# Order of weight splits, norms and the second token tile at the ten block borders, and of the scan's first phases, in a one-core transformer forward pass

## The reference, cut to what matters

```python
x = layer_norm(ALPHA * x + (1.0 + gate) * y, g, b)      # borders mla, mlp0, s5, mlp1
h = x * (1.0 + scale) + shift                           # what the next block reads
x = x + MACARON_WEIGHT * rms_norm_2(swiglu(rms_norm_2(x, pre_g), ...), post_g)   # ffn blocks
# s5: u = h @ w_in; complex recurrence over 256 steps, 64 groups x 64 states
a = exp((lr + i*li) * dt);  s[t] = a * s[t-1] + B u[t];  y[t] = Re(C s[t]) + d * u[t]
z = gelu(y); out = (z * sigmoid(z @ w_glu + b_glu)) @ w_out
```

## Time and profile before

| what | value |
|---|---|
| median of 3 runs (lowest, highest) | 1851.33 us (1848.64, 1853.93) |
| the profiled execution, its own time | 1848.97 us |
| its span, first to last instruction | 1847.2 us |
| mean granted TensorE clock | 0.942 of full speed |
| busy in the span: PE, DVE, ACT, POOL | 91%, 61%, 45%, 8% |

### The profile page before, as it was taken

One profiled execution on the slowest core, in us unless ns is written; L12 is line 12 of the kernel. 1 busy time (PEld: TensorE's weight loads), 2 busy tenths in 40 slices (PEclk: granted clock), 3 DMA queues, 4 the chain that ended last, 5 costly groups with the idle time before them and its releaser, 6 DMA issues.

```text
span 1847.2 us, 20552 instructions
## 1 busy us (share of the span) xinstructions
PE 1679.6 (91%) x8247; PEld 1350.5 (73%) x8247; DVE 1135.9 (61%) x1346; ACT 834.3 (45%) x1129; POOL 144.3 (8%) x293
## 2 busy tenths in 40 slices
PE   8778899984989899989999959999999999789998
PEld 3656688863668688868888747888788888568887
DVE  1876767893989756585455756544655455655444
ACT  2443455543234445544444675343544344554343
POOL 4320010012631010000000000000000000000000
PEclk9878899997999899989999979999999999889999
DMA  9658368853019466536654524555456555225552
GB/s 299 236 161 255 133 235 309 296 208 114 2 38 334 153 219 247 175 111 206 221 198 161 194 71 171 192 183 192 150 182 205 183 193 194 91 92 204 183 184 90
DMA packets 165496, 335.45 MB, mean 182 GB/s; under 512 B 38773, under 2 KB 54461, under 8 KB 164250
## 3 DMA queue, kind: packets, MB, share of 16 engines
q1 hardware_dynamic: 144602, 292.63, 46.8%
q0 software_dynamic: 9696, 37.29, 5.5%
q10 hardware_dynamic: 11104, 4.23, 0.9%
HBM read 328.86 MB, written 6.83 MB: 182 GB/s over the span
## 4 chain that ended last, share of the span: by engine, by line
PE 69%; DVE 19%; ACT 4%; issue 3%; DMA 2%; POOL 2%; SPq 1%; DVEq 0%; ACTq 0%; POOLq 0%
PE ps L635 21%; PE ps L637 21%; PE ps L636 21%; DVE wlo L1715 5%; PE ps L720 2%; PE ps L1157 1%; ACT whi L1186 1%; SPq L532 1%; DVE work L1757 1%; DVE xlo L1720 1%; DVE work L2148 1%; DMA work<-in_mod_mix_w 1%; DVE X L1849 1%; DMA operands<-in_mod_ffn_w 1%; DVE small L1780 1%
## 5 line engine op out<-in xcount | busy, mean ns | idle before, releaser
L1715 DVE TENSOR_TENSOR wlo<-raw,whi 128x2048 fp32r<-128x2048 f32 (+2 forms) x247 | 559.4, 2284 | 303.0 <-ACT whi L1186 302.4
L1186 ACT ACTIVATE whi<-raw 128x2048 fp32r<-128x2048 f32 (+2 forms) x247 | 465.7, 1906 | 233.2 <-PE ps L637 185.8
L635 PE MATMUL ps<-whi,xhi 128*128 128x512 f32 (+2 forms) x1244 | 486.2, 391 | 26.3 <-DVE wlo L1715 15.3
L636 PE MATMUL ps<-wlo,xhi 128*128 128x512 f32 (+2 forms) x1244 | 478.7, 385 | 0.0
L637 PE MATMUL ps<-whi,xlo 128*128 128x512 f32 (+2 forms) x1244 | 478.6, 385 | 0.0
L635 PE MATMUL ps<-whi,hhi 128*128 128x512 f32 x736 | 295.5, 402 | 23.8 <-DVE hlo L1720 23.3
L635 PEld LDWEIGHTS ps<-whi,xhi 128*128 128x128 f32 x1244 | 240.5, 193 | 73.6 <-DVE wlo L1715 17.7
L636 PE MATMUL ps<-wlo,hhi 128*128 128x512 f32 x736 | 289.4, 393 | 0.0
L637 PE MATMUL ps<-whi,hlo 128*128 128x512 f32 x736 | 289.4, 393 | 0.0
L637 PEld LDWEIGHTS ps<-whi,xlo 128*128 128x128 f32 x1244 | 239.8, 193 | 45.7
L636 PEld LDWEIGHTS ps<-wlo,xhi 128*128 128x128 f32 x1244 | 240.8, 194 | 43.4
(11 more groups left out here) (347 smaller groups left out, 1610.8 us busy)
## 6 DMA issues: line engine op xcount, KB each, us to landing
raw<-in_mlp_w SPq DMA_DIRECT2D x64, 1024.0 KB, 5.3
raw<-in_ffn_w_gate SPq DMA_DIRECT2D x44, 1024.0 KB, 5.1
raw<-in_ffn_w_up SPq DMA_DIRECT2D x44, 1024.0 KB, 5.1
raw<-in_ffn_w_down SPq DMA_DIRECT2D x44, 1024.0 KB, 4.9
mod<-in_mod_ffn_w POOLq DMA_DIRECT2D x16, 1024.0 KB, 7.1
mod<-in_mod_mix_w POOLq DMA_DIRECT2D x12, 1024.0 KB, 6.6
work<-in_mod_mix_w SPq DMA_DIRECT2D x8, 1024.0 KB, 9.0
operands<-in_mod_ffn_w SPq DMA_DIRECT2D x8, 1024.0 KB, 8.1
```

What stands on the lines that cost most here:

```text
L635: pe.matmul(o, lh, rh, start=start, stop=False)
L636: pe.matmul(o, lh, rl, start=False, stop=False)
L1186: act.activation(whi[:, c % SPL, 0:n], raw[:, c % RAW, 0:n], ACT.Copy).then_inc(hi_done, 1)
L1715: dve.tensor_tensor(wlo[:, c % RAW, 0:n], raw[:, c % RAW, 0:n], whi[:, c % SPL, 0:n].bitcast(F32), ALU.subtract).then_inc(lo_done, 1)
```

## The change

At each border the split of the next block's first chunk moves ahead of the norm of tile 0 on DVE (and on ACT where it was not so), that of the third chunk ahead of the norm of tile 1, and PE takes head 2 of tile 0 before it transposes tile 1. In s5 POOL makes the phases of duos 0 and 1 before it opens the three row tiles, DVE ends phase 0 and phase 1 around `residual`, ACT makes tables 0 and 1 between its token copies, and the split of chunk c+6 goes into the scan's loop. PE transposes the first token slice before it spreads a modulation row (`spread_third`, L723). SP loads the two norm rows behind chunk c+8 instead of c+5.

```diff
-                if name == "s5" and k == 5:
+                if name == "s5" and k == 8:
                     sp.wait_ge(res_ok, 4)
...
                     head(nxt, 1, 0)
+                    head(nxt, 2, 0)
                     turn(nxt, 1)
-                    head(nxt, 2, 0)
...
                 acc_ready("s5", 1)
+                token_turn("s5", 0, 0)
                 spread_third(6, (0, 1))
-                for tt in range(T):
-                    token_turn("s5", 0, tt)
+                token_turn("s5", 0, 1)
...
# ACT, leave
+                hi(n0)
                 if name in ("mla", "s5"):
                     despread(2 if name == "mla" else 8)
-                if name in LN_GLUES: hi(n0); glue(0)  else: glue(0); hi(n0)
+                glue(0)
...
                 x_hi(nxt, 0)
-                if name in LN_GLUES: hi(n0 + 2); glue(1)  else: glue(1); hi(n0 + 2)
+                hi(n0 + 2)
+                glue(1)
...
# DVE, leave
+                lo(n0)
                 glue(0)
                 if nxt:
-                    lo(n0)
+                    lo(n0 + 1)
                     x_lo(nxt, 0)
-                    lo(n0 + 1)
+                    lo(n0 + 2)
                 glue(1)
...
-                lo(n0 + 2)
                 x_lo(nxt, 1)
...
# ACT, s5 (table(i) is the body of the old loop over duos)
                 hi(c + 3)
+                table(0)
                 token_copy("s5", 0, 1, c + 1)
+                table(1)
                 despread(6)
                 hi(c + 4)
-                hi(c + 5)
                 for tt in range(T):
                     feature_copy("s5", 0, tt, uT)
+                hi(c + 5)
                 for tt in range(T):
                     token_copy("s5", 1, tt, c + 3)
-                hi(c + 6)
                 for tt in range(T):
                     feature_copy("s5", 1, tt, uT)
-                for i in range(DUOS):
+                for i in range(2, DUOS):
+                    if i == 3:
+                        hi(c + 6)
+                    table(i)
...
# DVE, s5
-                for j in range(3):
-                    lo(c + 3 + j)
-                residual(2)
-                lo(c + 6)
-                dve.wait_ge(feat_ok, FEAT0["s5"] + 4)
+                lo(c + 3)
...
                 phase(0)
+                residual(2)
                 phase(1)
+                lo(c + 4)
+                lo(c + 5)
+                dve.wait_ge(feat_ok, FEAT0["s5"] + 4)
                 for i in range(DUOS + 1):
+                    if i == 2:
+                        lo(c + 6)
...
# POOL
             pool.wait_ge(glue_done, 3)
+            s5_steps()
+            s5_phases(range(2))
             for f in (7, 8, 9):
                 open_third(f)
-            s5_phases()
+            s5_phases(range(2, DUOS))
```

More of the change, by code:

```diff
@@ L1491, in s5, with table @@
                 hi(c + 3)
-                token_copy("s5", 0, 1, c + 1)
-                despread(6)
-                hi(c + 4)
-                hi(c + 5)
[L1496 to L1499, removed]
-                hi(c + 6)
-                for tt in range(T):
-                    feature_copy("s5", 1, tt, uT)
-                for i in range(DUOS):
+                def table(i):
                     s = i % 3
@@ L1515, in s5 @@
                     act.activation(tabs[:, s, 0, :], half, ACT.Copy, scale=-2.0, bias=1.0).then_inc(table_ok, 1)
+                table(0)
+                token_copy("s5", 0, 1, c + 1)
+                table(1)
+                despread(6)
+                hi(c + 4)
+                for tt in range(T):
+                    feature_copy("s5", 0, tt, uT)
+                hi(c + 5)
+                for tt in range(T):
+                    token_copy("s5", 1, tt, c + 3)
+                for tt in range(T):
+                    feature_copy("s5", 1, tt, uT)
+                for i in range(2, DUOS):
+                    if i == 3:
+                        hi(c + 6)
+                    table(i)
                 yf = Y.rearrange("p t d -> p (t d)")
@@ L2408, in _, with s5_steps @@
             pool.memset(wide_row[:, :], 0.0).then_inc(s5p_pool, 1)
-            def s5_phases():
+            def s5_steps():
                 count = ph[:, 0, 0, 0:P].bitcast(I32)
@@ L2415, in s5_phases @@
                 do(pool.tensor_copy(iotaf, count))
-                for i in range(DUOS):
+            def s5_phases(duos):
+                for i in duos:
                     s = i % 2
```

## The result

The changed kernel takes 1801.01 us (median of 4 runs, 1798.16 to 1804.04) against 1850.47 us of the kernel before on the same chip. The ratio is 0.9731, with a 95% interval of 0.9709 to 0.9753. The forecast was 1800. The profiled execution of after took 1798.16 us, with a span of 1796.2 us and a mean granted clock of 0.959.

What follows compares the result with a forecast made beforehand. PE, busy 91% of the span, was taken as the bound, so only its stalls and slow stretches could go. Borders 34.7 plus scan 15, near 50 us off 1848.97, gave 1799, or 1801 on the median's scale; forecast 1800, range 1786 to 1816.

Steps and rivals of the forecast that it cites:

- The waits ahead of and behind turn 1: PE at borders: waits ahead covered for 9.4 us (RMS) and 10.2 us (layer norm), waits behind for 8.1 us.
- The clock at the RMS borders: Behind `turn` 1 of five borders: clock kept up, 11.7 us gained; rival that it stays low, 1812, chance 0.15.
- holes of 3.5 us did no harm: `turn` 0 of mlp1 to ffn10: a 3.5 us PE hole left the clock at 1.00, so shorter holes keep it.
- The layer-norm borders: Clock there: 2.6 us at stake at each border, 3.6 us taken together, bounds 0 and 8.
- The split paid in full at mlp0 and s5: DVE has no idle time ahead of norm 0 there, so the split costs its whole 2.28 us, 4.56 together.
- the point where I would be wrong: Sign against the forecast: `turn` 0 waiting longer than 2.3 us at any border.
- kv to ffn11: Border without any wait before: 0.8 to 1.2 us of the second tile's copy comes into the open, -1.0 us.
- The scan: Start of the scan in s5: x_rot of duo 0 at 447.6 instead of 467.16, near 15 us gained.
- its first point: What sets the scan's start: POOL, with duo 2 ready at 438.6, later than the features at 434.3.
- the chain on ACT: In s5, from `glue_done` at 410.4 through splits, phases, `residual`, table 1 and copies to last features at 434.3.
- the chunk held behind the norm rows: Ahead of the scan: SP held chunk c+6 behind norm rows waiting 18.8 us for `residual`, making PE's 17.1 us wait.
- this step: Scan's start: POOL beside DVE costs two duos 3 us, bounds 0 and 7; rival POOL late, 1809, chance 0.13.

Runs made afterwards that it cites:

- the sixth run: The changed kernel with all three duos' phases ahead of the row openings and DVE's `residual` moved behind phase 1: 1794.49 us, ratio 0.9705.
- the third run: The kernel before with one change, SP loading the two norm rows behind chunk c+8 instead of c+5: 1836.88 us, ratio 0.9933.
- the scan's part alone: The kernel before with all of the change except `cross` and the two `leave` functions, so borders as before: 1833.21 us, ratio 0.9913.

## Why the prediction was right, point by point

The time was right (1800 forecast, 1801.0 measured), by a sum of which most terms held and two had errors of opposite sign.

**The waits ahead of and behind turn 1** went as forecast: 14.4 to 2.4 us and 15.8 to 0.5. The estimate that some 0.8 us would stay for the second tile's input measured 0.88 to 1.04 us.

**The clock at the RMS borders** stayed up, which gave the five borders 24.1 us where 23.8 were forecast. The hole was the forecast one (2.1 us; 2.3 to 2.4 counted from matmul to matmul). The argument from it, that holes of 3.5 us did no harm, rested on one trace and does not hold: behind that very hole, `turn` 0 of mlp1 to ffn10, the clock was 0.72 in after, and the run with PE's old order has falls at two of five borders with holes of 3.3 to 3.8 us. What the runs do bear is narrower: behind 2.3 to 2.4 us it never fell at an RMS border.

**The layer-norm borders** gave 11.7 where 9.6 were forecast. Without the clock the forecast's terms are 1.4 us for mlp0 to s5 (2.75 + 0.9 - 2.28), 1.0 for s5 to mlp1 and 3.65 for mlp1 to ffn10. The marks give 3.3, 2.35 and 6.05, so 5.7 us are left for the clock, which was taken at 3.6. That is partly luck: in the traces where the clock falls behind `turn` 1 of mlp1 to ffn10, this border gains 2.5 to 2.8 us less. At the other two the longer first hole did bring part of the loss back, as forecast: from matmul to matmul at `turn` 0 it grew from 3.05 to 5.3 us and from 4.1 to 6.3, and the clock over the six microseconds behind it went from 1.00 to 0.72 and from 0.74 to 0.57. The split paid in full at mlp0 and s5 was right as to place: L1776 starts behind it at 384.65, and `turn` 0 waits 1.50 us, at s5 to mlp1 2.55. That is longer than the 2.3 us that I named as the point where I would be wrong, and the border still gained 2.35 us. The condition was too strict: what `turn` 0 lost there was less than what `turn` 1 gained.

**kv to ffn11** lost 1.25, forecast 1.0, and the run that undoes it gives it back.

**The scan** is the step with the wrong size: 11.8 us for 14.4 to 15. Three terms are off. The two first duos took 12.6 us where 7.3 + 3 was taken (bounds 0 and 7 for the 3; it was 5.3). The rows took 12.6 where 13.5 was taken, since two of them landed in 1.2 and 1.3 us and one in 4.7. And the loop lost 2.8 us where 1.7 was taken: "from there each duo costs what it did" was not so, because the ring of phases has settled into another rhythm, 11.4 us the pair for 11.1. On its first point the forecast named the right engine: duo 2 was ready at 434.8, 4.7 us behind the features. It also had the chain on ACT, with `residual` ahead of phase 1: 23.9 us from `glue_done` to the last features, and 25.0 measured. What it didn't ask is what that order costs, though it had written down that everything is queued behind table 1: 3.8 us of ACT's queue, which the sixth run takes back once duo 2 is out of the way.

**What the parts were worth.** The prediction explains the scan's gain by the chunk held behind the norm rows. The third run shows that to be all of it, or nearly: moved alone, the rows gain 11.4 of 11.6 us. The other edits of s5 bought 3.6 us at the scan's start and paid 2.3 of it back in its loop, and became worth something (6.9 to 8.8 us more by the marks) only with duo 2 and the residual in other places.

**POOL beside DVE.** The prediction named a page of the Trainium skill as speaking against this step. The rows above bear its rule out: 2.38 us beside one split, and 1.15 to 1.32 us for each POOL step beside a `residual` instruction of 1.28. By the rule ("SBUF — State Buffer", section "Who interferes with whom") the second duo half under `residual` would take four times 1.28 us, and it took 1.15 to 1.32 us each time: the trace agrees. It also says that POOL instructions that only write are not held, and the trace shows that too: a MEMSET took 0.95 us beside DVE's split of 2.28 us in the third run.

**What stays open.** The medians give the scan's part alone 17 us and the marks 10.5 from the end of mlp0 on. 3.5 of the rest lie in the first two blocks, where executions of one kernel differ by as much, and the two profiled executions differ by 13.7, not 17, so the remainder is scatter between executions as far as these runs can tell. What makes the first block differ, by what link the reordering changes the loop's rhythm, and what decides whether the clock falls behind a hole of 3.3 to 3.9 us or ahead of the scan, was not tried.

## What to carry to other kernels

When a pass is ready and an engine waits in front of a dependent step, put the pass there: it pays once for the wait and once more for the clock, if the hole that is left is short (2.3 us here). When a chain is moved to another engine's queue, follow who waits for it on every queue, to the end: here four DVE instructions stood ahead of a phase and slowed POOL besides, and ACT's queue paid. And test each edit of a bundle alone and with its neighbours: one number brought all of the scan's gain, one edit brought nothing alone and some 4 to 5.6 us behind another. Last, look at the clock of each trace before a gain is put down to an order: at two places of this program it came out both ways for the same code.

## What the hardware showed that I had not expected

- A POOL instruction of 0.37 us can be held over two DVE instructions in a row, not one: 4.53 us, from 424.31 to 428.84, beside two splits of 2.3 us that follow each other without a gap. Beside `residual`'s four, which also follow each other closely, each POOL instruction got in between two of them.
- A row of 4 KB lands with the chunk of 1 MB that is in flight: 1.2 us when that chunk was about to land, 4.5 us when the chunk had as long to go, so that issuing the row 2.8 us sooner gained nothing. After's third row, issued at 426.44, landed at 431.12, within 0.1 us of SP's second norm row.
- A hole in front of the same matmuls, 3.9 us long in 14 traces, had the granted clock at 0.72 behind it in six of them and at 1.00 in eight. Where it fell there, it did not fall at the next hole, and with the changed border that made it 2.5 to 2.8 us shorter.
- The two rhythms of the scan's loop, 5.4 and 5.7 or 5.0 and 6.4 us, are each stable over ten steps, and differ by 0.3 us a pair for the same instructions on the same ring. The second one stands in all nine traces with the reordered scan and two slots, the first in the three with the old order.
